# Two shared-expert products moved to the first expert pass, and the finish's transposes moved ahead of a tile's last contraction step

## What is computed

```python
def swiglu(x, w13, w2):
    a, b = jnp.split(x @ w13, 2, axis=-1)
    return (jax.nn.silu(a) * b) @ w2
...
    y = swiglu(h, w_sh13, w_sh2)                 # the shared expert
    for e in range(N_EXPERTS):
        y = y + combine[:, e:e + 1] * swiglu(h, w_exp13[e], w_exp2[e])
...
        h = layer_norm(DN_ALPHA * h + moe(h, ...), ln2_g[i], ln2_b[i])
        h = h + jax.nn.sigmoid(h @ w_ple_gate[i]) * (pe @ w_ple_in[i])
```

## Time and profile before

| what | value |
|---|---|
| median of 3 runs | 1343.71 us (1342.95, 1343.71, 1348.38) |
| the profiled execution, its own time | 1347.09 us |
| its span in the profile | 1345.4 us |
| mean granted TensorE clock | 0.963 |
| PE matmul busy | 1235.0 us, 92% |
| DVE / ACT / POOL busy | 634.0 / 243.5 / 457.1 us |
| expert loop, first up product to last scaling | about 643.6 to 1237.8 |
| finish, from the last scatter to the end | about 1238.6 to 1345.4 |

### The profile page before, as it was taken

The page is one execution under the profiler, slowest core; times in us unless marked ns, Lnnn a source line. Parts: engine busy times, 40 slices in busy tenths (PEclk is TensorE's granted clock), DMA queues, the critical chain, the costliest instruction groups (busy, mean ns, idle before and its releaser), DMA issues.

```text
span 1345.4 us, 20753 instructions
## 1 busy us (share of the span) xinstructions
PE 1235.0 (92%) x7495; PEld 516.8 (38%) x7495; DVE 634.0 (47%) x1099; ACT 243.5 (18%) x506; POOL 457.1 (34%) x574
## 2 busy tenths in 40 slices
PE   6999888999999898999799999898999988988997
PEld 3446443445545554544232223232322322222443
DVE  1335679969992443574323332333233332231875
ACT  1025241032255310111011101110110110101211
POOL 5435424412144100165444434244443433421010
PEclk9998989999989899999899999999999998989999
DMA  8224220122111248114799999999999999988961
GB/s 281 58 80 133 65 92 9 63 73 74 38 25 29 78 139 347 42 42 158 286 398 413 415 413 410 405 405 417 396 412 398 404 404 390 398 361 304 414 158 47
DMA packets 98106, 318.65 MB, mean 237 GB/s; under 512 B 51641, under 2 KB 53437, under 8 KB 80024
## 3 DMA queue, kind: packets, MB, share of 16 engines
q1 hardware_dynamic: 74432, 267.85, 51.6%
q0 software_dynamic: 22960, 47.45, 10.1%
q10 hardware_dynamic: 624, 2.12, 0.5%
HBM read 298.70 MB, written 31.33 MB: 245 GB/s over the span
## 4 chain that ended last, share of the span: by engine, by line
PE 56%; DMA 30%; DVE 7%; issue 2%; ACT 2%; POOL 2%; SPq 1%; POOLq 0%; DVEq 0%; ACTq 0%
DMA arena<-in_w_exp 24%; PE ps L1348 13%; PE ps L1697 11%; PE ps L1710 5%; PE ps L1627 4%; PE ps L1324 3%; DMA arena<-y_rows 3%; PE ps L1437 3%; PE ps L1487 2%; PE ps L1534 2%; DMA arena<-h_rows,arena 2%; PE ps L1467 1%; PE ps L1618 1%; PE ps L1337 1%; DMA arena<-in_w_in 1%
## 5 line engine op out<-in xcount | busy, mean ns | idle before, releaser
L1697 PE MATMUL ps<-arena 128*32 128x512 f32 x3072 | 355.6, 617 | 36.4 <-DMA arena<-in_w_exp 32.2
L2193 DVE STREAM_TRANSPOSE arena<-arena 128x1024 f32<-128x1024 f32 x48 | 99.8, 2080 | 254.3 <-DMA arena<-h_rows,arena 254.3
L1006 POOL DMA_INDIRECT arena<-h_rows,arena x192 | 193.0, 1005 | 67.9 <-issue 67.3
L1697 PEld LDWEIGHTS ps<-arena 128*32 128x32 f32 x3072 | 97.7, 113 | 263.4 <-issue 218.9
L1710 PE MATMUL ps<-arena 128*32 128x512 f32 x1536 | 173.6, 592 | 0.8 <-DVE arena L2214 0.8
L1348 PE MATMUL ps<-arena 128*128 128x512 f32 (+1 forms) x384 | 169.4, 600 | 4.4 <-DMA arena<-in_w_in 4.4
L1065 ACT ACTIVATE arena<-ps 128x512 f32<-128x512 f32 (+5 forms) x226 | 102.7, 486 | 373.2 <-PE ps L1324 206.3
L1013 POOL DMA_INDIRECT y_rows<-arena x48 | 48.7, 1015 | 304.0 <-DVE arena L2214 292.7
L1348 PEld LDWEIGHTS ps<-arena 128*128 128x128 f32 x384 | 73.7, 195 | 92.5 <-issue 91.8
L1710 PEld LDWEIGHTS ps<-arena 128*32 128x32 f32 x1536 | 49.8, 110 | 115.3 <-issue 115.3
L1279 ACT ACTIVATE arena<-ps 128x256 f32<-128x256 f32 x48 | 18.4, 383 | 381.3 <-PE ps L1697 381.3
(11 more groups left out here) (234 smaller groups left out, 1309.9 us busy)
## 6 DMA issues: line engine op xcount, KB each, us to landing
arena<-in_w_exp SPq DMA_DIRECT2D x64, 2048.0 KB, 23.2
arena<-in_w_exp SPq DMA_DIRECT2D x64, 1024.0 KB, 17.7
arena<-in_w_in SPq DMA_DIRECT2D x6, 2048.0 KB, 7.9
arena<-y_rows SPq DMA_DIRECT2D x5, 2048.0 KB, 12.7
arena<-y_rows SPq DMA_DIRECT2D x5, 1024.0 KB, 7.9
arena<-in_x_prompt SPq DMA_DIRECT2D x8, 512.0 KB, 6.5
arena<-in_cache_v SPq DMA_DIRECT2D x128, 32.0 KB, 1.7
arena<-in_w_out SPq DMA_DIRECT2D x2, 2048.0 KB, 8.1
```

Source lines behind the costliest of these rows:

```text
L1006: pool.indirect_dma_start(out=xg[s][:, 256 * g:256 * g + 256], out_offset=None, in_=h_quarters, in_offset=bass.IndirectOffsetOnAxis(ap=fro ...
L1697: ins = mm(ps[e % 2][q, :], xgT[e % 2][:, kk, q], w13[slots[g]][:, kk, :], start=(kk == 0), stop=(kk == KT - 1))
L2193: v.transpose(xgT[e % 2].rearrange("p c (g i) -> p g c i", g=4), xg[e % 3].rearrange("p (g j c) -> p g c j", g=4, c=KT)).then_inc(turned, 1)
```

## The change

Shared pieces 0 and 1 leave passes 12 and 15. Piece 0 goes ahead of `up_x(0)` on PE and piece 1 between `up_x(0)` and `turn_act(0)`; DVE adds both in pass 0, behind `turn_x(1)` and ahead of the two products. Pieces 2 to 8 stay where they were. In the finish, PE's eight transposes of tile `q + 1` move from behind tile `q`'s contraction to a place ahead of its very last step (`c == 1`, `k == 7`), for tiles 0 to 3. ACT's program is the same.

```diff
@@ -159,7 +159,8 @@
 
 
 SHARED_DOWN = [(t, c) for t in range(4) for c in range(2)] + [(4, 1)]
-SHARED_AT = {12 + 3 * n: n for n in range(len(SHARED_DOWN))}
+SHARED_FIRST = 2
+SHARED_AT = {12 + 3 * n: n for n in range(SHARED_FIRST, len(SHARED_DOWN))}
 
 
 def plan_banks():
@@ -1724,7 +1725,11 @@
             for e in range(PASSES):
                 if e in SHARED_AT:
                     shared_down(SHARED_AT[e])
+                if e == 0:
+                    shared_down(0)
                 up_x(e)
+                if e == 0:
+                    shared_down(1)
                 if e >= 1:
                     down_x(e - 1)
                 turn_act(e)
@@ -1779,7 +1784,8 @@
             pe.sem_inc(passed_pe, 1)
             pe.wait_ge(wpg_in, 32)
 
-            for q, t in enumerate(LAST_ORDER):
+            def turn_last(q):
+                t = LAST_ORDER[q]
                 r = ROWS[t]
                 pe.wait_ge(h2_ready, q + 1)
                 for i in range(2):
@@ -1789,6 +1795,10 @@
                         k = 4 * i + j
                         ins = nc.tensor.transpose(ps[4 + i][:, P * j:P * j + r], m[0:r, t, P * k:P * k + P], ident[0:r, 0:r])
                     ins.then_inc(h2_turned, 1)
+
+            turn_last(0)
+            for q, t in enumerate(LAST_ORDER):
+                r = ROWS[t]
                 pe.wait_ge(h2_read, 2 * q + 2)
                 if t == 4:
                     if q >= 2:
@@ -1803,6 +1813,8 @@
                     if n >= 4:
                         pe.wait_ge(sg_ready, n - 3)
                     for k in range(KT):
+                        if c == 1 and k == KT - 1:
+                            turn_last(q + 1)
                         ins = mm(ps[n % 4][0:r, :], h2T[q % 2][:, k, 0:r], wpg_parts[k // 4][:, k % 4, 512 * c:512 * c + 512], start=(k == 0), stop=(k == KT - 1))
                     ins.then_inc(gate_up, 1)
 
@@ -2219,6 +2231,9 @@
                     turn_x(e + 1)
                 if e in SHARED_AT:
                     add_shared(SHARED_AT[e])
+                if e == 0:
+                    for n in range(SHARED_FIRST):
+                        add_shared(n)
                 dve.wait_ge(sig_ready, e + 1)
                 if e >= 2:
                     dve.wait_ge(act_turned, e - 1)
```

## The result

The changed kernel takes 1347.14 us (median of 20 runs), the kernel before 1342.06 us beside it (median of 20): ratio 1.0045, 95% interval 1.0033 to 1.0057, so 6.0 us more (4.4 to 7.7). The two medians themselves are 5.1 us apart; differences are read from the ratios here. One ratio further down, of the loop's half with the gather first, leaves out an execution of 6372 us.

A forecast was written before the change was run, and what follows sets the result against it. Weight loads were taken to pace the loop, its end following the issue at 668.96, and PE with ScalarE the finish. Loop 4.5 plus finish 1.8 gave 6.3 us on a median of 1343.71, so 1350.0 us, range 1345 to 1355.

The forecast's parts named there:

- Loop, 4.5 forecast: Start of expert loop: shared product 1 and two adds delay the load issue of 668.96 and the loop's end, 4.5 us.
- The insert: Pass 0, before DVE's product L2225: add 0, shared product 1, add 1 in a row, 3.3 or 5.2 us; 5.2 taken.
- The doubtful price: Shared product 1 in pass 0: 1.88 us as in pass 12, or 3.82 us as at the finish's start; dearer taken.
- I take half: Pass 0, activation turning to down products: of 1.35 us lost to low clock, 0.7 us assumed to come back.
- Finish, 1.8 forecast: Finish, tiles 3 and 4: transposes ahead of the last contraction step lengthen the path, 1.8 us after a clock discount.
- The undiscounted sum: Finish: +1.96 us at tile 3 and +0.71 us at tile 4, together 2.67 us before any clock discount.
- Half off, 0.85: Finish, tile 3's contraction: half of its 1.70 us clock loss assumed to go, 0.85 us taken off.
- Passes 12 and 15, and product 0, at nothing: Removed products covered by weight waits; product 0 fits PE's 4.13 us idle before pass 0's up products; priced at nothing.
- ScalarE's order: Finish: copies stay behind a waiting sigmoid; if they overtook it, finish about -0.3 instead of +1.8 us, sum 4.2.
- Rival (a), gather early: Loop start: pass 1's gather lands before about 648, loop gains 3.7 us, sum -1.9 us, 1341.8 us; chance 0.08.
- (b), the loop swallows it: Loop: weight loads catch up behind 669, only the finish's cost is left, 1345.5 us; chance 0.12.
- (c), low clock everywhere: Product 1, pass 1's up products and a second finish contraction all cold: 11.1 us, 1354.8 us; chance 0.13.

The follow-up runs named there:

- loop's half with the gather first: Shared pieces moved into pass 0 as in the change, before's finish, SP waiting for pass 1's gather before further main-slot loads; against the kernel before: 0.9998.
- PE kept busy: Shared pieces moved as in the change, before's finish, six extra products on PE ahead of shared product 1; against the kernel before: 1.0030.
- loop's half alone: Changed kernel with before's finish, so only the shared pieces moved into pass 0; against the kernel before: 1.0029, +3.9 us.
- finish's half alone: Kernel before with only the finish's transposes moved ahead of the last contraction step; against the kernel before: 1.0012, +1.6 us.
- both in the idle time: Both shared products ahead of pass 0's up products, both adds behind the activation's products, before's finish; against the kernel before: 0.9999.
- the wait on SP: SP issues main-slot loads for the second pass on only after pass 1's gather lands; alone on the kernel before: 0.9975; with the change: 1.0057.
- five pieces: Five shared pieces instead of two in pass 0, before's finish; against the kernel before: 1.0076, +10.2 us.
- whole change with the gather first: The whole change plus SP waiting for pass 1's gather before further main-slot loads; against the kernel before: 1.0057, 7.7 us more.
- all together: Both products before pass 0's up products, adds behind activation's products, SP's gather wait, finish's transposes moved, ScalarE's copies before second sigmoid; against before: 0.9982.
- copies early: Finish's transposes moved as in the change, plus ScalarE's copies of the next tile ahead of the second sigmoid; against the kernel before: 1.0000.
- one more held: Both products before pass 0's up products, adds behind activation's products, SP's gather wait one load earlier, holding the kept slot's load; against before: 0.9998.

## Why the prediction was right

It said +6.3 us (0.47%); measured were +6.0 us (0.45%, with 4.4 to 7.7 us for the interval), by the mechanism forecast. The time it gave, 1350.0 us, lies 2.9 us above the measured median: it was built on the median of three runs, 1.65 us above that of twenty, and the two medians are 5.1 us apart. Two of its terms were a little off, in opposite directions; that their sum came out so close is in part luck.

- **Loop, 4.5 forecast.** The insert was put at 5.2 and measured 5.23. The doubtful price, 3.82 or 1.88 us for product 1, was taken from the right row: 3.75, and PE kept busy made it 1.96. Off was "I take half" of the 1.35 us of returned clock: all of it came back (7.32 instead of 8.68 us; clock 1.00 in 665 to 670). That makes 3.9, in the trace as in the time of the loop's half alone (interval 1.2 to 6.4). What there is to give back differs between executions: pass 1's up products of 7.07 us took 8.23 in the profile of before and 9.79 in that of the finish's half alone, whose issue at 29.3 leaves the insert a cost of only 2.0. In the profiles of before and of the change the loop behind the issue is 2.3 us shorter with the change; two profiles whose loop is before's differ by as much (569.6 and 566.9).
- **Finish, 1.8 forecast.** The undiscounted sum, 1.96 + 0.71 = 2.67, is what the change costs against a finish like that of most profiles: 19.70 - 17.07 = 2.63. Against the profile of before it is 0.94, as that one had lost 1.70 us to the clock. "Half off, 0.85" was taken from a loss that two of nine executions show. Weighted so, 2.67 - 2/9 x 1.70 = 2.3, an estimate, and with the loop's 3.9 it is 6.2 us; measured were 6.0. So 1.8 was near, but for a reason that the runs do not bear out: the change gave back a loss that before mostly does not have. The time of the finish's half alone, +1.6, has an interval too wide to tell 0.94 from 2.63.
- **Passes 12 and 15, and product 0, at nothing.** The run with both in the idle time agrees: 0.9999, within 2.5 us. The Trainium skill, TensorE: Matmul & The Clock Gate, section "HAM oscillation — how this bites in real kernels", speaks for keeping PE's gaps short. The gap filled ahead of pass 0 paid in the up products (7.07 us instead of 9.91) and not in the time.
- **ScalarE's order.** The copies began 1.40 us after their banks were turned, behind the sigmoid, and under the last step when ScalarE's order was changed. The Trainium skill, TensorE: Matmul & The Clock Gate, section "Architectural detail: the array is 16× 32×32, not 1× 128×128", calls that engine's queue strictly first in, first out. The rows agree: 1.40 us of waiting with the sigmoid in front, none without.
- **Rival (a), gather early:** it landed 12.10 us behind pass 0's transpose, before 12.17; not tested at its own point of 648, as the wait on SP brought it to 9.6 us at best with the change's order. **(b), the loop swallows it:** refuted by five pieces, and by the loop column of the table. **(c), low clock everywhere:** product 1 was slow, but pass 1 and the finish ran at full clock in the profile of the change. In five of the six profiles with the loop's insert pass 1's up products took 7.07 us; in that of the loop's half with the gather first they took 8.84, so it can happen.

## What to carry to other kernels

Filling idle time pays only where the engine's end is what the next wait needs; ask which operand lands last there, and put the filler into a wait that something else ends, or behind the work that the chain goes through, not ahead of it (the same four operations cost 3.9 us at one place and, within the noise, nothing at another). An engine with a fixed order turns a moved instruction into a wait for everything behind it, on the other engines too: moving transposes up without moving their readers only made the line longer. And a clock loss seen in one profiled execution need not be the usual one: before discounting a term by it, look for the same instructions in another profile.

## What was not expected of the hardware

The clock came back within the insert: of four products in the run with five pieces the first took 3.57 us and the next 1.96, 1.95 and 1.95, with 0.87 us of idle between them. The same instructions of tile 3 took 14.00 us or 15.70 from one profile to the next, and a few tenths of idle ahead of the transposes went with it: 1.79 us in the profile of before (15.70), 1.47 in that of both products in the idle time (14.00). But the idle time alone does not tell: in the orders with the finish's half, 1.75 us (whole change with the gather first) and 2.95 us (all together) went with no loss, 4.03 us (copies early) with one. And a gather's time goes by the loads in front of it: pass 1's rows stood ready 12.17 us behind pass 0's with the loads ahead (11.83 to 12.43 over the eight profiles without the wait), 8.47 to 10.13 with some held back, and 6.88 with one more held.
